# Stick-breaking attention in a hybrid decoder layer: values, transposes and scores of a step in one row, scores two steps ahead

## What is computed

```
z = q k^T / 8 + b_sb[head]
causal = k_pos < q_pos
log_keep = where(causal, log_sigmoid(-z), 0)
after = cumsum(log_keep, reverse) - log_keep
w = where(causal, exp(log_sigmoid(z) + after), 0)
o = w v
```

## Time and profile before

| | |
|---|---|
| median of 3 runs | 1251.48 us (1250.68 to 1251.56) |
| profiled execution, its own time | 1251.72 us |
| its span, first to last instruction | 1249.9 us |
| mean granted TensorE clock | 0.997 of full speed |
| PE busy | 1222.3 us (98%) |
| DVE busy | 501.7 us (40%) |
| ACT busy | 409.8 us (33%) |
| POOL busy | 505.0 us (40%) |
| steps of stick-breaking | some 628 to 709 us of the span |

### The profile page before, as it was taken

The page is one execution under the profiler, slowest core; times in us unless marked ns, Lnnn a source line. Parts: engine busy times, 40 slices in busy tenths (PEclk is TensorE's granted clock), DMA queues, the critical chain, the costliest instruction groups (busy, mean ns, idle before and its releaser), DMA issues.

```text
span 1249.9 us, 24817 instructions
## 1 busy us (share of the span) xinstructions
PE 1222.3 (98%) x10516; PEld 1190.3 (95%) x10516; DVE 501.7 (40%) x921; ACT 409.8 (33%) x684; POOL 505.0 (40%) x415
## 2 busy tenths in 40 slices
PE   8999999999999999999999999999999999999996
PEld 7999999999998999999988899999999999999995
DVE  4842323221116630456468522847943223221115
ACT  6422222222225342344445433345422221222220
POOL 1354445434445354221331533462255435434451
PEclk9999999999999999999999999999999999999998
DMA  6222221222213223302222474231222222222211
GB/s 223 85 73 97 101 99 68 101 93 93 93 60 136 83 94 119 102 35 103 77 78 86 151 248 159 69 140 59 73 101 69 99 101 82 86 93 93 93 60 69
DMA packets 29074, 123.25 MB, mean 99 GB/s; under 512 B 4442, under 2 KB 10610, under 8 KB 17394
## 3 DMA queue, kind: packets, MB, share of 16 engines
q1 hardware_dynamic: 28994, 122.09, 27.8%
HBM read 115.39 MB, written 6.67 MB: 98 GB/s over the span
## 4 chain that ended last, share of the span: by engine, by line
PE 89%; DVE 5%; ACT 2%; DMA 1%; DVEq 1%; POOL 1%; issue 1%; SPq 0%; POOLq 0%; ACTq 0%
PE bank L1455 28%; PE bank L1456 27%; PE bank L1457 27%; PE bank L1653 1%; DVEq L1088 1%; PE bank L1710 1%; PE bank L1695 1%; PE bank L1733 1%; PE bank L1682 1%; DMA va<-v_self 1%; PE bank L1719 1%; POOL w_lo L601 1%; DVE h L1127 1%; DVE u_lo L1105 1%; PE bank L1479 0%
## 5 line engine op out<-in xcount | busy, mean ns | idle before, releaser
L601 POOL TENSOR_TENSOR w_lo<-raw,w_hi 128x512 fp32r<-128x512 f32 x368 | 477.0, 1327 | 714.2 <-ACT w_hi L676 527.9
L1455 PE MATMUL bank<-u_hi,w_hi 128*128 128x260 f32 x1952 | 558.3, 286 | 3.1 <-ACT sg L805 2.3
L1456 PE MATMUL bank<-u_lo,w_hi 128*128 128x260 f32 x1952 | 551.0, 282 | 0.0
L1457 PE MATMUL bank<-u_hi,w_lo 128*128 128x260 f32 x1952 | 551.0, 282 | 0.0
L1455 PEld LDWEIGHTS bank<-u_hi,w_hi 128*128 128x128 f32 x1952 | 367.4, 188 | 12.3 <-issue 11.8
L1457 PEld LDWEIGHTS bank<-u_hi,w_lo 128*128 128x128 f32 x1952 | 367.6, 188 | 0.0
L1456 PEld LDWEIGHTS bank<-u_lo,w_hi 128*128 128x128 f32 x1952 | 367.5, 188 | 0.0
L676 ACT ACTIVATE w_hi<-raw 128x2048 fp32r<-128x2048 f32 x81 | 154.8, 1911 | 305.8 <-PE bank L1457 302.2
L1455 PE MATMUL bank<-hid_hi,w_hi 128*128 128x260 f32 x704 | 199.4, 283 | 1.1 <-POOL w_lo L601 1.1
L1456 PE MATMUL bank<-hid_lo,w_hi 128*128 128x260 f32 x704 | 198.9, 283 | 0.0
L1457 PE MATMUL bank<-hid_hi,w_lo 128*128 128x260 f32 x704 | 198.8, 282 | 0.0
(11 more groups left out here) (202 smaller groups left out, 1287.2 us busy)
## 6 DMA issues: line engine op xcount, KB each, us to landing
raw<-w_stream SPq DMA_DIRECT2D x84, 1024.0 KB, 4.9
raw<-w_stream SPq DMA_DIRECT2D x8, 768.0 KB, 4.7
e_raw<-w_stream SPq DMA_DIRECT2D x5, 1024.0 KB, 8.5
h<-x_t SPq DMA_DIRECT2D x4, 520.0 KB, 7.4
y_t<-h SPq DMA_DIRECT2D x8, 260.0 KB, 2.2
low<-kb_pool SPq DMA_DIRECT2D x8, 256.0 KB, 3.8
after<-vb_pool SPq DMA_DIRECT2D x8, 256.0 KB, 4.1
pair<-kb_pool SPq DMA_DIRECT2D x6, 256.0 KB, 3.7
```

Of the source, the lines that this page charges most:

```text
L601: return pool.tensor_tensor(low[:, a], src[:, a], top[:, a].bitcast(F32), ALU.subtract)
L1455: pe.matmul(out, w, hi_x, start=first, stop=False)
L1456: pe.matmul(out, w, lo_x, start=False, stop=False)
L1457: return pe.matmul(out, v, hi_x, start=False, stop=last)
```

## The change

PE's step becomes `b_apply(w - 1)`, `b_turn(w)`, `b_scores(w + 2)`, and behind them one whole item; `b_scores(1)` moves ahead of the loop, between the transposes of v and `fill(49)`. ACT's step becomes `item_out`, both `b_copy(w)`, `b_top(w - 1)`, both `b_sigmoid(w + 2)`, then the half split; `b_sigmoid(1)` goes ahead of the loop. DVE's chain in step w becomes that of w + 2, still with `b_low(w - 1)` in it, and the chains of 1 and 2 stand ahead of the loop. The work, its shapes, banks, buffers and semaphores are the same.

```diff
@@ ACT
             item_out(24)
+            b_sigmoid(1, 0)
+            b_sigmoid(1, 1)
             for w in range(PAIRS_B):
                 if w < 15:
                     item_out(25 + w)
-                if w + 1 < PAIRS_B:
-                    b_sigmoid(w + 1, 0)
+                b_copy(w, 0)
+                b_copy(w, 1)
                 if w:
                     b_top(w - 1)
-                if w + 1 < PAIRS_B:
-                    b_sigmoid(w + 1, 1)
-                b_copy(w, 0)
-                b_copy(w, 1)
+                if w + 2 < PAIRS_B:
+                    b_sigmoid(w + 2, 0)
+                    b_sigmoid(w + 2, 1)
                 if w % 4 >= 2:
                     hi_part(GA + 2 + w // 4, w % 4 - 2)
             b_top(PAIRS_B - 1)
@@ DVE
             b_chain(1)
+            b_chain(2)
             for w in range(1, PAIRS_B):
-                if w + 1 < PAIRS_B:
-                    b_chain(w + 1, w - 1)
+                if w + 2 < PAIRS_B:
+                    b_chain(w + 2, w - 1)
                 else:
                     b_low(w - 1)
@@ PE
             turn_v(4)
+            b_scores(1)
             fill(49)
             fill(50)
             fill(51)
             pe.wait_ge(v_placed, 13)
             for w in range(PAIRS_B):
-                if w + 1 < PAIRS_B:
-                    b_scores(w + 1)
+
                 if w:
                     b_apply(w - 1)
+                b_turn(w)
+                if w + 2 < PAIRS_B:
+                    b_scores(w + 2)
                 fill(2 * (FILL_A + 2 + w))
-                b_turn(w)
                 fill(2 * (FILL_A + 2 + w) + 1)
             b_apply(PAIRS_B - 1)
```

## The result

The changed kernel takes **1257.78 us** in the median of 5 runs (1256.59 to 1258.14); the kernel before, beside it, 1251.48. The ratio is 1.0051, 95% interval 1.004 to 1.0062: slower by about 6.3 us, where 2.0 was forecast. The profiled execution has a span of 1256.0 us.

The account below looks back on a forecast made before the run. The prediction took PE's own stream to bound the kernel. Passages between kinds of work 2.05, less 0.2 for a vanished wait, plus 0.15 for new waits, gave 2.0 us more: 1253.5 us, range 1251.9 to 1256.0.

Parts of the forecast that it names:

- The joints: PE's passages between products, scores, values and transposes: fixed cost 8.60 us before, 10.65 after, so 2.05 us more.
- The fixed 0.71 a step: Fixed cost of PE's passages between kinds of work in each full step, 1 to 13: 0.71 us, 0.15 more than before.
- the sum: The forecast's added terms: 2.05 us for passages on PE, less 0.2 for step 15, plus 0.15 for new waits: 2.0 us.
- The unseen joint: PE passing from values through transposes to scores: transposes to scores costs 0.18 us beyond the transposes' own time, bounds 0 and 0.21.
- Rivals 3: Faster: one break a step instead of two, the row otherwise streams on; 1248.3 us, chance 0.04.
- rival 4: Costs less: each change of array shape costs only its first gap, 0.09 us; 1252.5 us, chance 0.09.
- The wait that goes: PE's 0.2 us wait for its weights in step 15 vanishes with scores two steps ahead: 0.2 us back.
- The steps with 4 blocks of scores: Values wait for DVE's low part after 4-block scores (w = 1, 5, 9, 13): slack 0.02 us.
- the signal: Delay from the end of DVE's low part to PE's start at the values, taken as 0.06 us.
- The steps with 3 blocks: Values wait for DVE's low part after 3-block scores (w = 4, 8, 12): slack 0.37, less 0.3 for GpSimd's split, 0.07 us.
- Rival 2: Slower: DVE's low part comes late by one delay d, so PE waits at values; 1254.0 to 1256.6 us, chance 0.25.
- 0.3 at each: Upper bound on PE's wait for DVE's low part at each of ten steps, 3 us together.

Follow-up runs that it names:

- run with two banks: Changed kernel with the values alternating between two PSUM banks, waiting for the low part of two steps back, same result: 1253.19 us, ratio 1.0015.
- short: Changed kernel with GpSimd's low parts of four weight chunks cut to 128 of 2048 columns: 1253.69 us; same cut on the kernel before: 1250.98 us.
- the early: Changed kernel with ACT making both halves of a chunk's high part in one step, so GpSimd's split starts about a step sooner: 1255.35 us, ratio 1.0031.
- cut split: Changed kernel with GpSimd computing only 1536 of 2048 columns of the low parts of four weight chunks: 1254.18 us, ratio 1.0021.

## Why the prediction was wrong

**What bounds the kernel:** right. PE's stream sets the end, and the stretch's 6.11 us are the kernel's 6.3 within what a run can tell.

**The joints:** right, term by term. The fixed 0.71 a step stands in the timeline after to 0.01 at each joint. Net of what step 15 no longer waits (0.13, below) the sum said 2.05 - 0.13 = 1.92; the run with two banks has 1.66. The 0.26 between them lies in no one joint: the first four full steps are 0.62 longer than before (from 3 blocks of scores to the next such, 20.81 against 20.19), 0.155 each as forecast, the next four 0.56 and the four after only 0.47 (20.78 against 20.31), as the kernel before itself takes 0.12 more there. Some 0.1 is left for the edges, cause open. The unseen joint, transposes to scores, took 0.58 where the sum has 0.36 + 0.05 + 0.18 = 0.59. Rivals 3 and 4 are out, rival 4 by the 0.23 behind scores and the 0.58.

**The wait that goes:** right in kind, and a little less than taken. Step 15 has 705.23 to 705.48 between the last product and the transposes before, 0.25 where a product's distance is 0.12, so 0.13 went and not 0.2.

**The steps with 4 blocks of scores:** slack 0.02 forecast, 0.10 short measured, four times: 0.4 us. One term accounts for it: the signal. The sum took 0.06, read where the transposes wait for DVE's weights; the values that wait for a low part start 0.14 to 0.15 behind its end, at all seven in the kernel after and at every such wait with the short, the early and the cut split. That is 0.09 more. The sum's 4.06 for the low part was right (4.07), and PE is ready at 4.12 (run with two banks) where it had 4.14.

**The steps with 3 blocks: here the forecast failed.** The step is the one that reads "I take 0.3 off: 0.07". The slack ahead of it, 0.37, was nearly right: 0.25 by the run with the short split, the 0.12 between them being mostly the same signal. The 0.3 was wrong: it is 1.6. I read the cost of GpSimd from where it falls in the kernel before, on one keep, and did not redraw when it falls. Moving DVE's chains one step ahead put the running products, the multiplication and the next mask under the same split, four operations of DVE in a row instead of a pause of 3.0 us, a mask, a keep and a part of the products. "GpSimd does not meet the chains of 4 blocks" was true and beside the point: it meets the chain of 2 blocks and the head of the one of 3.

**Rival 2** (chance 0.25) was thus the right mechanism with too small a size: the time lies 1.2 us above its own range, which ended at 1256.6. "The steps with 4 blocks of scores first" was wrong too: those with 3 blocks lose ten times as much. Its formula used one delay for all ten steps and ended at d = 0.4; the delays were 0.12 for four steps, 1.4 for three and none above 0.3 for the other three. With each its own: 4 x 0.10 + 3 x 1.34 = 4.4 instead of the 0.15 in the sum. With the measured joints, 1251.48 + 1.66 + 4.4 = 1257.5; measured 1257.78. The bound of 3 us for all ten steps was drawn from "0.3 at each", which no row carried. A bound for DVE's operations beside GpSimd would have been the worst price in the rows for each one under the split: 1.36 for the keep against the 0.43 that it takes clean is 0.93, four operations make 3.7, and less DVE's pause of some 2.1 (known only from the run with the short split) that is the 1.6 measured.

**What is shown and what is argued.** Shown: the waits are GpSimd's doing (short split), they act through the one bank (two banks), they follow the split when it moves, and they set in at a threshold. The 0.1 at the 4-block steps goes away with the second bank and stays with the short split, so it is the low part without GpSimd; that its size is the signal's is read from the starts, and no run changed the signal. Which shared part of the chip makes DVE and GpSimd slow each other, no run shows.

## What to carry to other kernels

When a change shifts one engine's work by a step, lay its new timeline over what the other engines do at that time; the cost of two engines side by side belongs to the overlap and not to the operation on which it was last seen. A slack smaller than the largest such cost is no slack. And where two stages share one bank, a second bank is the cheapest insurance: here it gave back 4.5 of the stretch's 6.1 us. Even then this row cost 1.7 us more than the old order; only the row with the scores first came level with it.

## What the runs showed of the hardware

**GpSimd beside DVE costs per operation.** Each of the two running products of 256 elements went from some 0.7 to 1.6 us, a multiplication of 512 from 0.69 to 1.56, a mask of 256 from 0.42 to 1.51, a keep of 512 from 0.43 to 1.35: about 0.9 to 1.1 more for each, whatever its own length. GpSimd's four went from 5.37 to 6.23 us together. The low part, which reads one operand from a PSUM bank, took 0.29 also in the middle of the split (652.07 before). This has the form of turns taken, an instruction at a time (a single one of GpSimd's lasts 1.28 at least), and not of shared speed. The run with the cut split bears it out: there GpSimd's instructions are shorter (384 columns, 1.01 at least), and the two running products and the multiplication take 1.34, 1.42 and 1.27 us instead of 1.61, 1.69 and 1.56, so the price follows the length of GpSimd's instruction. The turns are not strict end to end: the clean times of the two products, the multiplication, the mask and the split's four add up to 1.39 + 0.69 + 0.42 + 4 x 1.28 = 7.6 us, and side by side they are done in 6.50 (648.85 to 655.35). The Trainium skill, SBUF — State Buffer, section Who interferes with whom, has such a rule: DVE and GpSimd share a pair of ports under an exclusive lock held for a whole instruction; a DVE instruction with two SBUF inputs contends with a GpSimd one that reads SBUF, and so does one in a 2-port performance mode, which `tensor_scalar` can enter. The traces agree for the running products, the multiplication and the mask, which have two SBUF inputs and pay 0.9 to 1.1 us each, and for the low part, which has one and pays nothing. The keep has one SBUF input too and pays 0.9 all the same; it is a `tensor_scalar`, and no row shows its mode.

**Waiting values start 0.15 us behind the instruction that frees their bank.** From the end of DVE's low part to the start of the values it is 0.14 to 0.15 us in every such wait of six traces (the kernel after, the three with another split, the scores over 128 rows, the scores first), where the transposes started 0.06 behind DVE's weights. A slack counted with the wrong one of the two is off by 0.09.

**Two heads' scores on different halves of the array run side by side.** With 64 rows each, the records of the two heads start 0.01 us apart (635.23 and 635.24 in the kernel after) and a block of both heads costs 0.21 us; over 128 rows they start 0.43 apart (634.08, 634.51) and a block costs 0.42, with 0.12 fixed. The change of shape that the 64 rows bring is paid back from the first block on: ahead of values one block costs 0.21 + 0.42 with it and 0.12 + 0.54 without. The Trainium skill, TensorEngine Tiling (Array Packing), section Key Properties, states that tiles work independently and may compute in parallel; the rows agree.
